# Taking one semaphore wait away from the 5.6 MB table copy in a hybrid attention block

## The chip, the cores and the metric

The kernel runs on one core of one Trainium2 chip. The metric is the device time of one execution in microseconds (us); lower is better. All work is float32: the large products are made as three products of split operands (high times high, high times low, low times high).

## The reference, cut to what matters

One decoder layer over 512 positions of width 1024. A conditioning vector gives shift, scale and gate; a normalised, modulated input `h` goes through one wide projection `w_in`, whose columns feed three attention branches; these are gated, merged, projected, and a SwiGLU mixer follows.

```python
c_act = jax.nn.silu(c)
mod = (c_act @ w_ada[l] + b_ada[l])[:, None, :]
sh1, sc1, gt1, sh2, sc2, gt2 = jnp.split(mod, 6, axis=-1)
h = rmsnorm(x, g_norm1[l]) * (1 + sc1) + sh1
(a_q, a_kv, i_q, i_k, i_w, b_q, b_k, b_v, c_q, c_k, c_v,
 z_a, z_b, z_c) = split_cols(h @ w_in[l], IN_SPLITS)
...
bias = jnp.moveaxis(bias_tab[rel_bucket(dist)], -1, 0)
logits = jnp.einsum('bqhmd,bshmd->bmhqs', qb, k) * ATTN_SCALE + bias
```

The bias depends only on the distance of query and key. So a table of a head is one row of values, laid out so that each partition reads it shifted by one.

## The kernel before, in words

**The program.** Each engine has its own instruction stream, and they meet at semaphores. SyncE (SP) issues nearly all loads, GpSimd (POOL) the few constants and the bias rows. The order on each engine is written out by hand.

**Weights.** Weights come in chunks of 1 MB (`w_raw`, two buffers, 1024 rows of 1 KB each). For each chunk ScalarE makes the high part (`make_hi`, L1143), VectorE the low part (`make_lo`, L1438), and TensorE multiplies (`project`, L762 to L764). A buffer is loaded anew (L504) when the low part of the chunk that was in it is made. Chunk 0 is the first column block of `w_in` that is used, chunks 1 to 5 follow, and chunk n+2 takes the place of chunk n. Chunk 2 is smaller (two loads).

**The start.** SP issues, without a wait: six small vectors (L510), `x` in two loads (L512), sixteen loads of 512 KB of `w_ada` (L517), chunk 0, chunk 1. All these are in one hardware queue and are worked off in order. VectorE sums the `w_ada` rows scaled by `c_act` (L1457), TensorE turns the sums into columns (L780), and then:

- ScalarE: `make_hi(0)`, then the eight high parts of `h` (L1173), then `make_hi(1)`
- VectorE: `make_lo(0)`, then shift and scale columns, then for each of eight slices of `h` the full value (L1473) and its low part (L1478, which raises `h_ready`), then `make_lo(1)`
- TensorE: tile 0 of chunk 0, slice by slice as `h_ready` rises, then the other tiles of chunks 0, 1 and 2, then chunk 3

So neither `h` nor the first projection begins before chunk 0 has landed.

**The bias tables.** TensorE makes 24 rows by a small product with a one-hot matrix (L791), ScalarE copies them to SBUF (`brow`, L1166). POOL stores them in DRAM as one flat row of 11264 values (`row_dram`, four DMAs, L676) and waits until they have landed. Then it copies that row 128 times in DRAM (`rep_dram`, L680, 5.6 MB, one DMA in the software queue). Much later, from L550 on, SP reads tables out of the copies with a pitch of one row less one element. The next instruction of POOL after the copy is `power(2, ...)` (L669), which serves the key latents.

Of the kernel before, what the change touches and what calls it, by code (L numbers as in the profile page):

```python
# [25 lines left out]
KT = D // P  # L26
# [171 lines left out]
def hybrid_block(nc, a, out):  # L198
# [7 lines left out]
    def sem(name):  # L206
        return ctx.enter_context(nc.semaphore(name))

    with ctx:
# [175 lines left out]
        h_ready = sem("h_ready")  # L385
# [262 lines left out]
        def _(pool):  # L648
# [27 lines left out]
                pool.dma_start(row_dram[0, f0:f0 + n * w].rearrange("(n w) -> n w", w=w), brow[r0:r0 + n, c0:c0 + w]) \  # L676
                    .then_inc(rows_stored, 16)
            pool.wait_ge(rows_stored, 16 * 4)
            pool.wait_ge(h_ready, KT)
            pool.dma_start(rep_dram, row_dram.to_broadcast([P, FL_W])).then_inc(rows_copied, 16)  # L680
            power(2, rs_kv, ms_kv, 4)

# [59 lines left out]
        def _(pe):  # L742
# [243 lines left out]
            def project_z(v):  # L986

                if chunk_starting_at(v) is not None:
                    chunk_ready(chunk_starting_at(v))
                (_, n), kts = dense_at(v)  # L990
                project((CH_Z + n // 2) % 2, ATT_TILE["z", n], h_hi, h_lo, [(k, k) for k in kts], n % 2 * P,
                        first=0 in kts, last=KT - 1 in kts)
# [938 lines left out]
```

## Time and profile before

| what | value |
|---|---|
| runs | 1055.12, 1054.15, 1052.42 us |
| median | 1054.15 us |
| profiled execution, own time | 1055.12 us |
| its span | 1053.0 us |
| TensorE busy | 1000.0 us, 95% |
| VectorE, ScalarE, GpSimd busy | 484.5, 412.4, 115.7 us |
| mean granted TensorE clock | 0.983 |
| moved by the DMA engines | 121.49 MB |

The profile is of one execution. "PE" is TensorE, "DVE" VectorE, "ACT" ScalarE. The span runs from the first to the last instruction; the execution's own time has 2.1 us more around it. The whole kernel is one stream of TensorE work after about 45 us, so a time at which TensorE starts or stalls counts more than the busy share of any other engine.

### The profile page before, as it was taken

How to read it: one execution, taken by the hardware profiler on the slowest of the kernel's cores; microseconds unless marked ns; L12 is line 12 of the kernel's file. 1: busy time of each engine (PE TensorE's matmuls, PEld its weight loads, DVE VectorE, ACT ScalarE, POOL GpSimd, SP SyncE). 2: the span in 40 equal slices, each digit the busy share in tenths (PEclk: the TensorE clock that was granted, in tenths of full speed). 3: DMA queues.
4: the chain of work that ended last, by engine and by line, in shares of the span. 5: the costliest groups of instructions: out<-in, count | busy, mean ns of one | idle time of the engine just before them, and what ended most of it. 6: DMA issues, size and time to landing. Idle time of an engine off the chain costs nothing.

```text
span 1053.0 us, 12662 instructions
## 1 busy us (share of the span) xinstructions
PE 1000.0 (95%) x4831; PEld 809.4 (77%) x4831; DVE 484.5 (46%) x803; ACT 412.4 (39%) x676; POOL 115.7 (11%) x136
## 2 busy tenths in 40 slices
PE   2799999999999999999999999799999999999997
PEld 0677988878877766778888888588888888788886
DVE  3845687833235344553746567623233232322331
ACT  4434523255455655642222222433344433412231
POOL 3000000000044411200000026300000000001111
PEclk9799999999999999999999999899999999999999
DMA  8693134312130201155556583032322323223302
GB/s 305 223 295 119 51 116 139 113 48 81 61 102 21 72 21 31 34 177 175 169 176 211 197 282 115 3 120 80 120 80 81 118 84 115 70 80 110 110 31 80
DMA packets 93262, 121.49 MB, mean 115 GB/s; under 512 B 4680, under 2 KB 83109, under 8 KB 93090
## 3 DMA queue, kind: packets, MB, share of 16 engines
q1 hardware_dynamic: 92690, 114.67, 33.0%
q0 software_dynamic: 528, 6.22, 2.0%
q8 instruction: 29, 0.48, 0.2%
q14 instruction: 15, 0.12, 0.0%
HBM read 118.20 MB, written 8.45 MB: 120 GB/s over the span
## 4 chain that ended last, share of the span: by engine, by line
PE 86%; DMA 4%; DVE 4%; ACT 2%; SPq 2%; issue 1%; POOL 0%; POOLq 0%; DVEq 0%; ACTq 0%
PE tile_ps L762 24%; PE tile_ps L764 23%; PE tile_ps L763 23%; DMA w_raw<-in_w_in_dram 4%; PE s_ps L902 2%; PE t_ps L920 2%; PE o_ps L949 2%; SPq L517 2%; DVE w_lo L1438 1%; ACT w_hi L1143 1%; PE s_ps L905 1%; PE tile_ps L963 1%; PE tile_ps L1008 1%; PE tile_ps L969 1%; PE tile_ps L1009 1%
## 5 line engine op out<-in xcount | busy, mean ns | idle before, releaser
L762 PE MATMUL tile_ps<-h_hi,w_hi 128*128 128x512 f32 x816 | 326.9, 401 | 13.1 <-DVE h_lo L1845 4.3
L764 PE MATMUL tile_ps<-h_hi,w_lo 128*128 128x512 f32 x816 | 320.3, 393 | 0.0
L763 PE MATMUL tile_ps<-h_lo,w_hi 128*128 128x512 f32 x816 | 319.9, 392 | 0.0
L1438 DVE TENSOR_TENSOR w_lo<-w_raw,w_hi 128x2048 fp32r<-128x2048 f32 (+2 forms) x78 | 172.3, 2209 | 249.0 <-ACT w_hi L1143 249.0
L762 PEld LDWEIGHTS tile_ps<-h_hi,w_hi 128*128 128x128 f32 x816 | 153.9, 189 | 58.2 <-issue 16.7
L764 PEld LDWEIGHTS tile_ps<-h_hi,w_lo 128*128 128x128 f32 x816 | 153.9, 189 | 33.5
L1143 ACT ACTIVATE w_hi<-w_raw 128x2048 fp32r<-128x2048 f32 (+2 forms) x78 | 143.8, 1844 | 89.9 <-PE tile_ps L764 68.7
L763 PEld LDWEIGHTS tile_ps<-h_lo,w_hi 128*128 128x128 f32 x816 | 154.3, 189 | 29.9
L762 PE MATMUL tile_ps<-f_hi,w_hi 128*128 128x512 f32 x176 | 69.1, 393 | 2.5 <-DVE f_lo L1862 2.5
L764 PE MATMUL tile_ps<-f_hi,w_lo 128*128 128x512 f32 x176 | 69.2, 393 | 0.0
L763 PE MATMUL tile_ps<-f_lo,w_hi 128*128 128x512 f32 x176 | 69.1, 393 | 0.0
L1266 ACT ACTIVATE nl<-nl,cst 128x256 f32<-128x256 f32 (+3 forms) x81 | 43.0, 532 | 55.4 <-DVE cst L1609 55.3
L1401 ACT ACTIVATE f_hi<-f_t 128x512 f32 x22 | 13.9, 633 | 95.5 <-DVE f_t L1858 95.5
L722 POOL TENSOR_TENSOR sq_acc<-x 128x512 f32<-128x512 f32 x2 | 2.1, 1042 | 442.2 <-DVE x L1872 267.6
L693 POOL TENSOR_TENSOR tm<-tab,score 128x256 f32<-128x256 f32 (+2 forms) x24 | 24.4, 1015 | 175.1 <-DVE cst L1609 175.1
L1858 DVE TENSOR_TENSOR f_t<-tile_ps,silu_t 128x512 f32<-128x512 f32 x22 | 15.2, 692 | 60.2 <-PE tile_ps L764 60.2
L1278 ACT ACTIVATE pt<-t_ps 128x128 f32<-128x128 f32 (+2 forms) x80 | 32.1, 402 | 27.1 <-PE t_ps L920 26.5
L762 PEld LDWEIGHTS tile_ps<-f_hi,w_hi 128*128 128x128 f32 x176 | 33.5, 190 | 9.8 <-DVE f_lo L1862 2.9
L764 PEld LDWEIGHTS tile_ps<-f_hi,w_lo 128*128 128x128 f32 x176 | 33.4, 190 | 7.0
L763 PEld LDWEIGHTS tile_ps<-f_lo,w_hi 128*128 128x128 f32 x176 | 33.4, 190 | 7.0
L1396 ACT ACTIVATE silu_t<-tile_ps 128x512 f32<-128x512 f32 x22 | 13.2, 600 | 46.2 <-PE tile_ps L764 46.1
L1609 DVE CUSTOM_DVE_ANT_0 nl<-s_ps,tm 128x256 f32<-128x256 f32 (+2 forms) x24 | 13.4, 557 | 36.6 <-PE s_ps L902 36.4
(272 smaller groups left out, 1354.1 us busy)
## 6 DMA issues: line engine op xcount, KB each, us to landing
w_raw<-in_w_in_dram SPq DMA_DIRECT2D x31, 1024.0 KB, 5.5
w_raw<-in_w_gate_up_dram SPq DMA_DIRECT2D x22, 1024.0 KB, 5.1
ada<-in_w_ada_dram SPq DMA_DIRECT2D x16, 1024.0 KB, 5.7
ada<-in_w_ada_dram SPq DMA_DIRECT2D x16, 512.0 KB, 15.4
w_raw<-in_w_down_dram SPq DMA_DIRECT2D x8, 1024.0 KB, 5.2
row_copies<-row_flat POOLq DMA_DIRECT2D x1, 5632.0 KB, 21.2
w_raw<-in_w_out_dram SPq DMA_DIRECT2D x4, 1024.0 KB, 9.6
tab<-row_copies SPq DMA_DIRECT2D x12, 256.0 KB, 2.7
```

The lines of the kernel that those rows point to most:

```text
L517: sp.dma_start(ada1[g][k][:], a["w_ada"][0][k * P:(k + 1) * P, g * D:(g + 1) * D]) \
L693: pool.tensor_tensor(tm[v % 2][:, 0:w], table_of(v), score[:, off:off + w], ALU.add) \
L762: pe.matmul(tile_ps[b][0:mw, :], wh, x_hi[:, kx, :], start=start, stop=False)
L763: pe.matmul(tile_ps[b][0:mw, :], wh, x_lo[:, kx, :], start=False, stop=False)
L764: mm = pe.matmul(tile_ps[b][0:mw, :], wl, x_hi[:, kx, :], start=False, stop=stop)
L902: mm = pe.matmul(ps[:, 0:w], qlat[h % 2][:, i * P:(i + 1) * P], kv_T[:, 0:w], start=True, stop=True)
L920: mm = pe.transpose(t_ps[v % 2][:, j * P:(j + 1) * P], src[:, j * P:(j + 1) * P], ident[:])
L949: mm = pe.matmul(o[:, i * P:(i + 1) * P], kv_nat[:, j, :], p_j, **flags)
L1143: nc.scalar.activation(w_hi[s][:, 0:kt, :], w_raw[s][:, 0:kt, :], ACT.Copy).then_inc(w_hi_made[s], 1)
L1266: act.activation(b, b, ACT.Exp, bias=negmax[:, k:k + 1], scale=-1.0, accum_out=expsum[:, k:k + 1]).then_inc(exped, 1)
L1278: act.activation(pt[v % 2][:, 0:w], t_ps[v % 2][:, 0:w], ACT.Copy).then_inc(pt_ready, 1)
L1438: dve.tensor_tensor(w_lo[s][:, 0:kt, :], w_raw[s][:, 0:kt, :], w_hi[s][:, 0:kt, :].bitcast(F32), ALU.subtract) \
```

## The change

The copy of the flat row no longer waits until all eight slices of `h` are ready. It is issued as soon as the four stores of the row have landed.

```diff
             pool.wait_ge(rows_stored, 16 * 4)
-            pool.wait_ge(h_ready, KT)
             pool.dma_start(rep_dram, row_dram.to_broadcast([P, FL_W])).then_inc(rows_copied, 16)
             power(2, rs_kv, ms_kv, 4)
```

## Rows read from the trace of the kernel before

**Rows 1.** The page: busy time; chain by engine; loads of `w_in`, KB, us to landing.
```profile
PE 1000.0 (95%) x4831; PEld 809.4 (77%) x4831; DVE 484.5 (46%) x803; ACT 412.4 (39%) x676; POOL 115.7 (11%) x136
...
PE 86%; DMA 4%; DVE 4%; ACT 2%; SPq 2%; issue 1%; POOL 0%; POOLq 0%; DVEq 0%; ACTq 0%
...
w_raw<-in_w_in_dram SPq DMA_DIRECT2D x31, 1024.0 KB, 5.5
```

**Rows 2.** Chain of waits, 0 to 140 us: start, duration, what.
```profile
20.52 17.63 DMA w_raw<-in_w_in_dram
...
40.12 2.29 DVE w_lo L1438
42.74 0.56 DVE x_T L1473
...
55.25 22.39 DMA w_raw<-in_w_in_dram
...
81.96 0.50 PE tile_ps L762
```

**Rows 3.** Timeline: start, duration, instruction, idle time before and its releaser.
```profile
26.61 2.30 POOL L676 DMA_DIRECT2D row_flat<-brow  x4 [6.02 <-ACT brow L1166]
...
38.18 1.91 ACT L1143 ACTIVATE w_hi<-w_raw 128x2048 fp32r<-128x2048 f32 x1 [4.75 <-DMA w_raw<-in_w_in_dram]
...
44.82 0.76 PE L762 MATMUL tile_ps<-h_hi,w_hi 128*128 128x512 f32 x1 [4.18 <-DVE h_lo L1478]
...
51.00 1.90 ACT L1143 ACTIVATE w_hi<-w_raw 128x2048 fp32r<-128x2048 f32 x1
...
52.36 0.55 POOL L680 DMA_DIRECT2D row_copies<-row_flat  x1 [23.45 <-DVE h_lo L1478]
```

**Rows 4.** The four row stores, L676, by their line.
```profile
L676 POOL DMA_DIRECT2D row_flat<-brow x4: 499/521/777, 26.6 to 28.4; - x4
...
DMA to landing us min/median/max: 4.6/4.7/5.0
```

**Rows 5.** The copy, L680, by its line.
```profile
DMA to landing us min/median/max: 21.2/21.2/21.2
```

**Rows 6.** DMA queue, 34.4 to 42 us: packets, MB, share of 16 engines.
```profile
q1 hardware_dynamic: 1772, 1.78, 73.7%
```

**Rows 7.** DMA queues, 53 to 71.9 us.
```profile
q0 software_dynamic: 128, 5.77, 92.3%
q1 hardware_dynamic: 80, 0.08, 5.5%
```

**Rows 8.** Hardware queue, 71.9 to 75 us, then 75 to 76.2 us.
```profile
q1 hardware_dynamic: 508, 0.52, 82.1%
...
q1 hardware_dynamic: 439, 0.44, 105.8%
```

**Rows 9.** TensorE's waits, 20 to 180 us: total, times, longest.
```profile
PE tile_ps L762 <- DVE h_lo L1478: 4.2, 1, 4.2
PE o_ps L780 <- DVE ada_sum L1457: 2.7, 1, 2.7
PE tile_ps L762 <- DVE w_lo L1438: 1.4, 1, 1.4
```

**Rows 10.** Timeline of ScalarE, 60 to 110 us.
```profile
70.18 0.59 ACT L1183 ACTIVATE iq_split<-tile_ps 64x512 fp32r<-64x512 f32 x1
77.66 1.92 ACT L1143 ACTIVATE w_hi<-w_raw 128x2048 fp32r<-128x2048 f32 x1 [6.89 <-DMA w_raw<-in_w_in_dram]
...
109.87 0.28 ACT L1217 ACTIVATE junk<-o_ps 128x128 f32<-128x128 f32 x1
```

**Rows 11.** Stages: length, busy time of each engine, granted clock, DMA share, GB/s.
```profile
44.00:48.00 4.00, 3.18 (x8) 2.53 (x9) 4.00 (x8) 2.36 (x4) 0.00 (x0) 0.50 0.76 194
48.00:49.00 1.00, 1.00 (x4) 0.79 (x3) 1.00 (x3) 0.63 (x1) 0.00 (x0) 0.63 0.00 0
```

**Rows 12.** Timeline of SyncE's queue, the first read of the copies.
```profile
175.35 2.34 SPq L550 DMA_DIRECT2D tab_near<-row_copies  x1
```

## The prediction

> **What bounds the kernel now.** I read the page first. TensorE is busy 95% of the span, and 86% of the chain that ended last is TensorE's [rows 1]. For almost any change outside TensorE the answer would then be "nothing". The exception is the time before TensorE has anything to multiply, and the removed wait acts just there. So I went next to the chain of waits of the first 140 us. The reader is to see two transfers in it [rows 2]. The load of chunk 0 is issued at 20.52 and lands 17.63 us later, at 38.15. Its high part, low part, the first slice of `h` and TensorE's first product follow without a gap: 38.18, 40.12, 42.74 and 44.82 [rows 2, 3]. The second is the load of chunk 3, issued at 55.25, which takes 22.39 us and lands at 77.64; TensorE starts on that chunk at 81.96. TensorE's waits of this stretch say what each costs: it waited 4.2 us for `h` at the start, and 1.4 us for the low part of chunk 3 [rows 9]. From there to 180 us it waited for nothing else.
>
> Third come the DMA queues, stretch by stretch. They show what the copy does to a load that is in flight with it. From 53 to 71.9 us the software queue, which then holds only the copy, works off 128 packets of 45 KB, 8 on each of the 16 engines. The hardware queue, which has chunk 3 waiting since 55.25 and chunk 4 behind it, works off 80 packets of 1 KB, 5 on each engine [rows 7]. A DMA engine that has both queues takes about one packet from each in turn, and one of 45 KB against one of 1 KB is no sharing at all. A packet of the copy occupies its engine 0.923 x 18.9 / 8 = 2.18 us. When the copy is through, the 1 KB packets move at full speed: 508 in the 3.1 us in which the last engines leave the copy, then 439 in 1.2 us, or 366 per us [rows 8]. This is why chunk 3 took 22.39 us.
>
> **The change part by part.** It removes a wait and adds nothing. What moves is one DMA issue.
>
> Step 1, when the copy is issued. The last of the four stores is issued at 28.4 and lands 4.7 us later (4.6 to 5.0), at 33.1 [rows 4]. The copy goes out then instead of at 52.36 [rows 3], which is 19.3 us earlier. Before, its first packets ran some 1.3 to 2 us after the issue (issue 52.36, all 128 start between 53 and 71.9 us [rows 7]). So they now begin at about 34.4, and it lands 21.2 us after the issue [rows 5], at 54.3.
>
> Step 2, what it meets. At 34.4 the hardware queue still has 1772 packets to send [rows 6]. Two chunks are 2 x 1024 packets of data and 2 x 16 that signal, 2080 together, so 308 are gone and chunk 0 has 1040 - 308 = 732 left, 46 for each engine. The `w_ada` packets are ahead of these and are through.
>
> Step 3, what chunk 0 gets. While the copy runs, one packet for each of the 8 packets of the copy on each engine: 128. Left over are 604. I move the rows of before by the 19.3 us. At 71.9 - 19.3 = 52.6 us the copy's packets have all started; 508 go in the next 3.1 us and the other 96 in 0.3 us, so the data ends at 56.0. For chunk 3 the same sum gives 960 packets left at 71.9, hence an end at 76.2 us, and it landed at 77.64: 1.4 us from the last data to landing. Chunk 0 lands at 57.4. If the slow 3.1 us are an accident and the 604 go at 366 per us, the data ends at 54.3 and it lands at 55.7. I take 57.2, close to the measured stretch. Against 38.15 that is 19.0 us late, with 17.5 and 19.3 as the ends.
>
> Step 4, what is behind it. `make_hi(0)` stands ahead of the high parts of `h` on ScalarE, and `make_lo(0)` ahead of the shift, scale and `h` work on VectorE, so all of it moves by the same 19.0 us: TensorE starts its first tile at 44.8 + 19.0 = 63.8. The cover for the lateness of chunk 0 is zero, since the chain runs through it [rows 2]. The sum for the two `w_ada` halves, for which TensorE waited 2.7 us [rows 9], ends before 41 us as before and no longer matters. TensorE's clock was granted at 0.50 from 44 to 48 us (the lower of 1.2 and 2.4 GHz) and rose between 48 and 49, about 3.8 us after TensorE had started [rows 3, 11]. It now stands idle for longer before the start, and the clock cannot be lower. I put no change on this. If it rises 2 us sooner or later after the start than it did, TensorE works 2 us more or less at half the rate, which is 1 us either way.
>
> Chunk 1 is next in the queue: 1040 packets at 366 per us are 2.8 us, landing at about 60. ScalarE wants it at 51.0 + 19.0 = 70.0 [rows 3]. Nothing waits there.
>
> Step 5, what the change gives back. Chunk 3 is now issued at 55.25 + 19.0 = 74.3, when the copy is 20 us gone, and takes some 5.5 us, the median of the loads of `w_in` [rows 1]. ScalarE can make its high part as soon as it is through with L1183, at 70.8 on the old clock, instead of at 77.66 [rows 10], VectorE the low part 4 us later, before TensorE is done with chunk 2. The 1.4 us of waiting [rows 9] go. Nothing else of the start was waiting for a transfer [rows 9], so this is the whole gain. It can be nothing at worst, if TensorE then meets another wait at that place.
>
> Step 6, downstream. The tables are first read at 175.35 [rows 12], 100 us after the copy had landed; making it earlier is worth nothing there. POOL's `power(2)`, which stands behind the copy, waits for squares that ScalarE makes at 109.87 [rows 10]. No slack after 64 us takes up a late start: TensorE works through, and its loads follow its own pace.
>
> Sum: +19.0 - 1.4 = +17.6 us. Ends: 17.5 - 1.4 - 1 = +15.1, and 19.3 - 0 + 1 = +20.3. The profiled execution took 1055.12 us, which gives 1072.7; it is the slowest of three, and the median is 1054.15. I forecast against the median: 1071.8, with ends at 1069.3 and 1074.5, and 2 us more on the low side and 1.5 on the high side for the runs' own spread of 2.7 us.
>
> **The rivals.**
>
> Several small packets in one turn. Chunk 3's packets were sent one to a turn [rows 7], but they were queued after the copy had begun. Chunk 0's are in the queue ahead of it, and may be fetched in groups. From six to a turn on it matters, since 46 are then through before the 8 turns are. At twelve to a turn, four turns of the copy (8.7 us) and the 46 packets' own 2.0 us come first: data to 45.1, landed at 46.5, +8.4 - 1.4 = +7.0, or 1061. Against it: 80 packets to 96 of the copy that ran beside them. The Trainium skill, "DMA: Bandwidth & Descriptors", section "Queues, rings and completion order", says that an engine goes round the queues by whole packets of typically 9 to 17 descriptors. By that rule, if each small record of this trace is one descriptor, chunk 0 would need six turns down to three, and the estimate is +11 to +5 us. The trace does not agree with such groups for the 1 KB rows. Chance 0.08.
>
> Sharing by bytes. If the engines gave each queue half of the bytes, chunk 0's 732 packets (2.0 us alone) would take 4.0 us: +2.0 - 1.4 = +0.6, or 1054.8, no change. What speaks for it is only that chunk 3's case began the other way round. Against it are 5.77 MB to 0.08 MB [rows 7]. Chance 0.05.
>
> The other side: chunk 0 is not held up at all, because its 46 packets on each engine are already taken in when the copy's first one comes. Then only the stall at chunk 3 goes: -1.4, or 1052.8, within what can't be told from no change. This decides from 46 packets taken in ahead on every engine, at which point the whole 17 us fall away; some ten would change little. No row shows how far an engine takes in ahead. Chance 0.04.
>
> That the copy isn't earlier after all: the wait on `h_ready` ended 23.45 us of POOL's idling [rows 3], and the stores behind it had long landed [rows 4], so it was what held the copy. Chance 0.01.
>
> **How the numbers follow.** The forecast has 0.82, the rivals 0.08, 0.05, 0.04 and 0.01. The range of 1067 to 1076 is the forecast's own and leaves out less than 2 in 10. About 0.3%, 3.2 us, is what a measurement of this kernel tells from no change. Slower by more than that are the forecast and the first rival, 0.90; within it the two small cases and the last, 0.09; faster 0.01, for a gain beyond the 1.4 us that I can't name.
>
> **What would show it.** The copy's issue at about 33 us instead of 52; 128 large packets from about 34 to 53 us, and in that stretch of the order of 130 small ones in the hardware queue (step 3; 700 would mean the second or third rival, some hundreds the first); ScalarE's wait for chunk 0 grown from 4.75 us [rows 3] to about 24; TensorE's first product at about 64; chunk 3 landing some 5.5 us after its issue, and no wait of TensorE for its low part (step 5); the distance from TensorE's first product to the end shorter by 1.4 us. I would be wrong most of all if an engine holds many packets of one queue in hand, or if the copy itself ran at another speed against a full queue.

## The result, and the profile after

The changed kernel takes 1066.3 us in the median of 4 timed runs (1062.2 to 1067.9); the kernel before, beside it, 1053.99 (1052.42 to 1055.12). The ratio is 1.011, with a 95% interval of 1.008 to 1.0141: slower by 12 us. The direction was forecast (slower, 0.90). The size was not: 1071.8 was forecast, with 1067 to 1076 as the range, and the median lies 0.7 us below it. The spread is also new: all 14 executions of this kernel in that job lie between 1060.65 and 1069.22.

The profiled execution took 1068.17 us, one of the slower ones, against 1055.12 for the one of before. Its chain of waits (start, duration, what), beside [rows 2]:

```profile
20.13 34.88 DMA w_raw<-in_w_in_dram
55.03 1.92 ACT w_hi L1142
56.98 2.29 DVE w_lo L1437
59.59 0.56 DVE x_T L1472
...
61.68 0.77 PE tile_ps L761
```

The load of chunk 0, 17.63 us before, takes 34.88 us and lands at 55.01 instead of 38.15, 16.9 us late. The steps behind it have their old lengths, and TensorE's first product comes at 61.68 instead of 44.82 [rows 3], 16.9 us late as well. (Lines past the edit are one lower than before.)

The waits of TensorE from 0 to 180 us, beside [rows 9]: the wait for `h` is 17.2 us longer, and the 1.4 us for the low part of chunk 3 is gone.

```profile
PE tile_ps L761 <- DVE h_lo L1477: 21.4, 1, 21.4
...
PE o_ps L779 <- DVE ada_sum L1456: 2.6, 1, 2.6
```

The timeline of POOL, beside [rows 3], and the copy's row among the DMA issues of 0 to 120 us (KB, us to landing), beside [rows 5]. The copy goes out at 32.97 and takes 22.8 us instead of 21.2:

```profile
26.23 2.29 POOL L676 DMA_DIRECT2D row_flat<-brow  x4 [6.02 <-ACT brow L1165]
32.97 0.54 POOL L679 DMA_DIRECT2D row_copies<-row_flat  x1 [4.46 <-DMA row_flat<-brow]
```

```profile
row_copies<-row_flat POOLq DMA_DIRECT2D x1, 5632.0 KB, 22.8
```

Now the DMA queues, stretch by stretch: 34.5 to 38, then 38 to 54, then 54 to 55.2 us. The first line of a stretch has all packets and how many are small; those under 512 B are signal packets, by which an engine reports that its share of a load is through, 16 for a load.

```profile
DMA packets 882, 1.59 MB, mean 455 GB/s; under 512 B 15, under 2 KB 866, under 8 KB 866
q1 hardware_dynamic: 866, 0.87, 78.8%
q0 software_dynamic: 16, 0.72, 48.7%
...
DMA packets 224, 5.16 MB, mean 323 GB/s; under 512 B 0, under 2 KB 112, under 8 KB 112
q0 software_dynamic: 112, 5.05, 96.0%
q1 hardware_dynamic: 112, 0.11, 3.7%
...
DMA packets 136, 0.12 MB, mean 103 GB/s; under 512 B 15, under 2 KB 136, under 8 KB 136
q1 hardware_dynamic: 122, 0.12, 34.4%
```

How the 16.9 us become 13.05. The first L825 transposes, behind the first tile of chunk 3, start at 102.8 (87.6 before): +15.2, so 1.7 us came back at chunk 3. The distance stays 15.2 up to 400 us and is 13.2 at the first transposes of the output (1053.3, L1121, against 1040.1). TensorE waits there for the same things and as long, to 0.3 us; what differs is the granted clock. These are the stretches in question, kernel before, then after (length, busy times, granted clock, DMA share, GB/s):

```profile
380.00:400.00 20.00, 18.10 (x82) 12.49 (x81) 10.52 (x33) 10.99 (x28) 2.89 (x5) 0.92 0.13 41
...
917.00:925.00 8.00, 6.26 (x21) 5.02 (x22) 3.66 (x4) 2.43 (x2) 0.00 (x0) 0.79 0.21 66
```

```profile
395.00:415.00 20.00, 18.10 (x93) 12.81 (x94) 10.71 (x33) 11.60 (x29) 2.87 (x5) 1.00 0.14 41
...
930.00:940.00 10.00, 7.53 (x34) 5.91 (x33) 4.28 (x4) 2.43 (x2) 0.00 (x0) 1.00 0.19 67
```

The execution of before had two short drops of the clock; the one of after had none there. They are not tied to the change: another profile of the changed kernel (the first one below) has both drops, with a granted clock of 0.91 from 395 to 415 us and 0.83 from 920 to 930 us. These 2 us are luck of the profiled pair.

### The profile page after: what moved, and what is told of

Its sections match the earlier page's. It is cut to its first block, busy times and chain, and to the rows that moved or that the text cites. A ratio compares the mean times of both kernels' runs of the same rounds, so it can differ in the third digit from the quotient of the medians.

```text
span 1066.2 us, 12661 instructions
## 1 busy us (share of the span) xinstructions
PE 997.5 (94%) x4831; PEld 808.3 (76%) x4831; DVE 484.5 (45%) x803; ACT 412.5 (39%) x676; POOL 115.5 (11%) x136
## 4 chain that ended last, share of the span: by engine, by line
PE 88%; DMA 3%; DVE 2%; ACT 2%; SPq 2%; issue 1%; POOL 0%; POOLq 0%; DVEq 0%; ACTq 0%
PE tile_ps L761 25%; PE tile_ps L763 24%; PE tile_ps L762 24%; DMA w_raw<-in_w_in_dram 3%; PE s_ps L901 2%; PE o_ps L948 2%; PE t_ps L919 2%; SPq L517 1%; PE s_ps L904 1%; PE tile_ps L962 1%; PE tile_ps L1007 1%; PE tile_ps L968 1%; PE tile_ps L1008 1%; PE tile_ps L1009 1%; DVE w_lo L1437 1%
## 5 line engine op out<-in xcount | busy, mean ns | idle before, releaser
L1857 DVE TENSOR_TENSOR f_t<-tile_ps,silu_t 128x512 f32<-128x512 f32 x22 | 15.2, 692 | 60.2 <-PE tile_ps L763 60.2
L1395 ACT ACTIVATE silu_t<-tile_ps 128x512 f32<-128x512 f32 x22 | 13.2, 600 | 46.3 <-PE tile_ps L763 46.2
L1608 DVE CUSTOM_DVE_ANT_0 nl<-s_ps,tm 128x256 f32<-128x256 f32 (+2 forms) x24 | 13.4, 557 | 36.6 <-PE s_ps L901 36.5
## 6 DMA issues: line engine op xcount, KB each, us to landing
row_copies<-row_flat POOLq DMA_DIRECT2D x1, 5632.0 KB, 22.8
```

The source lines that it names most:

```text
L1857: dve.tensor_tensor(f_t[:, m, :], tile_ps[m][:], silu_t[:, m, :], ALU.mult) \
```

## The experiments

**Theory A**, formed on the profile after: it is a race. The copy's first packets come several us after its issue, when the hardware queue is full. What an engine has not sent of a load by then goes out at one packet a turn, 2.2 us each. The load lands with the engine that is furthest behind. **Theory B** is the prediction's: hundreds of packets of chunk 0 are left at the copy's start, on all engines.

**The changed kernel again.** No edit. Two more profiles of it, besides that of the result.

> The changed kernel once more, unaltered. Theory A (the race of the last packets): in the profile of the changed kernel 15 of the 16 signal packets of chunk 0 were sent before the copy's first packets, and one engine's only after its last. Whether and how long chunk 0 is held is then decided by the engine that is furthest behind, and it lands between turns of the copy: at 38 us if all engines are through, else at about 38 + 2.2 n, up to 55 to 56. So I expect another landing of chunk 0 in this profile than 55.0 with even chance, the first product of TensorE 6.65 us after it, and a spread of the times of several us against under 3 for the kernel before. Theory B (the prediction's: hundreds of packets of chunk 0 are left when the copy begins): chunk 0 always lands 1 to 3 us behind the copy, within 1 us from run to run.

> The changed kernel once more, for a third profile of it. Theory A: chunk 0 lands between 38 and 56 us at a turn of the copy (two profiles showed 42.9 and 55.0), chunk 1 always 1 to 3 us behind the copy's last packets, near 59; the time is about 1061 if chunk 0 lands within the first three or four turns, since chunk 1 then sets it, and above that goes up with the landing of chunk 0 to 1069. A landing of chunk 0 behind the copy's end with hundreds of its packets left would speak for theory B.

The first: 1065.2 us in the median, runs of 1061.37, 1061.38, 1069.03 and 1069.25 against 1050.56 to 1056.03 for 19 runs of the kernel before. Timeline of ScalarE (chunk 0, chunk 1), then TensorE's waits:

```profile
42.88 1.91 ACT L1142 ACTIVATE w_hi<-w_raw 128x2048 fp32r<-128x2048 f32 x1 [9.31 <-DMA w_raw<-in_w_in_dram]
59.08 1.92 ACT L1142 ACTIVATE w_hi<-w_raw 128x2048 fp32r<-128x2048 f32 x1 [3.29 <-DMA w_raw<-in_w_in_dram]
```

```profile
PE tile_ps L761 <- DVE h_lo L1477: 8.0, 1, 8.0
...
PE tile_ps L761 <- DVE iq_split L1494: 3.4, 1, 3.4
```

The second (1061.5 us), the same rows, and its DMA packets of 34.5 to 38 and of 38 to 40 us:

```profile
39.21 1.91 ACT L1142 ACTIVATE w_hi<-w_raw 128x2048 fp32r<-128x2048 f32 x1 [6.58 <-DMA w_raw<-in_w_in_dram]
58.10 1.91 ACT L1142 ACTIVATE w_hi<-w_raw 128x2048 fp32r<-128x2048 f32 x1 [5.98 <-DMA w_raw<-in_w_in_dram]
```

```profile
PE tile_ps L761 <- DVE iq_split L1494: 6.0, 1, 6.0
PE tile_ps L761 <- DVE h_lo L1477: 5.9, 1, 5.9
```

```profile
DMA packets 797, 1.51 MB, mean 430 GB/s; under 512 B 15, under 2 KB 781, under 8 KB 781
...
DMA packets 32, 0.74 MB, mean 368 GB/s; under 512 B 1, under 2 KB 16, under 8 KB 16
```

One kernel, and chunk 0 lands at 55.0, 42.9 and 39.2. In the last case too 15 signals are out when the copy begins, but the 16th goes with the next turn. In the middle one it goes with the second turn, between 41.5 and 42 us. Theory B is dead: it had chunk 0 behind the copy each time. The profiles also show what the prediction had not seen. When chunk 0 gets through early, chunk 1 does not; it lands at 58 to 59 instead of 41, and TensorE waits 3.4 or 6.0 us for it (the row names VectorE's last instruction before; ScalarE's row above shows the DMA). So +4.7 us at the first product is +6.4 behind chunk 3, and +1.0 is +8.3.

**The copy twice.**

```diff
             pool.dma_start(rep_dram, row_dram.to_broadcast([P, FL_W])).then_inc(rows_copied, 16)
+            pool.dma_start(rep2_dram, row_dram.to_broadcast([P, FL_W])).then_inc(copied_again, 16)
```

> The copy is made a second time, into another DRAM tensor, straight behind the first; the tables wait for both. The software queue is then full of 45 KB packets for some 40 us instead of 20. Theory A: the engine that was behind has only a few packets of chunk 0 more than the turns of one copy, so chunk 0 lands between 55 and 72 us, before the second copy (about 76), and chunk 1, of which every engine has 65 packets left, lands behind the second copy at about 78 to 80. Theory B: each engine has 38 packets of chunk 0 left after the first copy and gets 8 more sent during the second, so chunk 0 lands at 76 to 78, some 21 us later than now, and the kernel takes about 1088.

1081.01 us in one run. Chunk 0 and chunk 1 on ScalarE:

```profile
54.78 1.91 ACT L1146 ACTIVATE w_hi<-w_raw 128x2048 fp32r<-128x2048 f32 x1 [22.55 <-DMA w_raw<-in_w_in_dram]
77.16 1.91 ACT L1146 ACTIVATE w_hi<-w_raw 128x2048 fp32r<-128x2048 f32 x1 [9.46 <-DMA w_raw<-in_w_in_dram]
```

(The edit also gives the second copy its tensor and its semaphore, for which the first read of the tables waits.) As A said, and not B: the second copy did not move chunk 0, which had hardly a packet more to send than the first copy had turns, and moved chunk 1 by some 19 us. (54.8 and 77.2 are a little under A's lower ends of 55 and 78. In this profile 13 signals of chunk 0 were out when the copy began, not 15: three engines had some left.)

**Holding the copy back.** One or two small power operations of POOL ahead of the issue.

```diff
             pool.wait_ge(rows_stored, 16 * 4)
+            for n in range(2):      # in the other kernel: once
+                pool.tensor_tensor(spare, ones[:, 0:4], half[:, 0:4], ALU.pow).then_inc(idled, 1)
+                pool.wait_ge(idled, n + 1)
             pool.dma_start(rep_dram, row_dram.to_broadcast([P, FL_W])).then_inc(rows_copied, 16)
```

> Between the landing of the row stores and the issue of the copy POOL makes two small power operations on a spare column, some 3 to 4 us in all, so the copy is issued at about 36.5 instead of 33. Theory A: by the time of its first packets every engine is through with chunk 0, which lands at 38.2 as in the kernel before, TensorE's first product is at 44.8; the engine furthest behind in chunk 1 is caught instead, chunk 1 lands at about 58 to 60 instead of 41, its low part is ready some 4 us after TensorE wants it at 58.5, and 1.4 us come back at chunk 3: about +3, or 1057. Theory B: the copy is 3.5 us later, so chunk 0 still has more than a hundred packets left and lands 1 us after the copy, at 58: about +17, or 1071.

> The copy is issued after one small power operation of POOL, at about 34.5 to 35, between the changed kernel (33, chunk 0 caught by one engine) and the kernel with two such operations (36.1, nothing caught). Theory A (the race): the first packets come at 38 to 38.5, every engine is through with chunk 0, which lands at 38 (a late engine may cost a turn or two, 2.2 us each), and chunk 1, of which 20 to 40 packets are left on each engine, lands behind the copy at 57 to 59. TensorE then waits some 7 us before the first tile of chunk 1 and no more for chunk 3: +6 to +8 in all, 1060 to 1062, with a spread as small as that of the kernel before. Rival (chunk 0's delay and chunk 1's go together, both set by the traffic of the copy): chunk 0 lands at a turn between 40 and 57 as before and the time is 1061 to 1069.

(`spare` and `idled` are a column and a semaphore made for this.) With two: issue at 36.14, chunk 0 at 37.4, and no wait of ScalarE for chunk 1, which was expected to be caught and was not. The time is 1053.77 (10 runs), a ratio of 0.9994 (0.9981 to 1.0008). The step that I had wrong was again when the copy's first packets come: between 38.5 and 40, when chunk 1 was sent too. How they come says why they are late. These are the stretches 38.5 to 39, 39 to 39.5 and 39.5 to 40 us of this kernel:

```profile
DMA packets 145, 0.49 MB, mean 985 GB/s; under 512 B 8, under 2 KB 137, under 8 KB 137
q0 software_dynamic: 8, 0.36, 170.0%
...
DMA packets 59, 0.32 MB, mean 637 GB/s; under 512 B 6, under 2 KB 53, under 8 KB 53
q0 software_dynamic: 6, 0.27, 126.1%
...
DMA packets 14, 0.10 MB, mean 201 GB/s; under 512 B 2, under 2 KB 12, under 8 KB 12
q0 software_dynamic: 2, 0.09, 41.9%
```

The 16 signals of chunk 1 come as 8, 6 and 2, and so do the copy's first 16 packets. An engine starts on the copy when it is through with all that it had of chunk 1, without taking turns for what was queued ahead. Against an empty queue (below) the copy's packets were there some 1.3 us after the issue, which here is 37.4; every engine first sent what it had in hand. (That the 8, 6 and 2 are the same engines is read from the counts; the trace doesn't name them.)

With one: issue at 35.06, first packets from 38.5 on, 1062.72 us (1061.58 to 1063.66), 0.7 us above what I expected, ratio 1.0096 (1.0077 to 1.0116). Seven engines were through with chunk 1 too (7 signals from 38.5 to 39.5). Its ScalarE rows and TensorE's first wait:

```profile
37.82 1.91 ACT L1146 ACTIVATE w_hi<-w_raw 128x2048 fp32r<-128x2048 f32 x1 [4.79 <-DMA w_raw<-in_w_in_dram]
58.15 1.91 ACT L1146 ACTIVATE w_hi<-w_raw 128x2048 fp32r<-128x2048 f32 x1 [7.42 <-DMA w_raw<-in_w_in_dram]
```

```profile
PE tile_ps L765 <- DVE iq_split L1498: 7.6, 1, 7.6
```

Chunk 0 on time, chunk 1 caught, and 1.1 us between the issues of the two kernels are worth 9 us. Four runs of the one lie within 2.1 us. Why a wait of 3.4 us costs less than one of 6 or 7.6 is in the granted clock, from 66 to 68 us in this kernel and in the first repetition (the number behind the five busy times):

```profile
66.00:68.00 2.00, 2.00 (x6) 1.54 (x6) 1.64 (x3) 1.15 (x1) 0.00 (x0) 0.50 0.45 160
```

```profile
66.00:68.00 2.00, 1.50 (x7) 1.29 (x8) 1.73 (x3) 1.98 (x2) 0.00 (x0) 1.00 0.94 333
```

After the 7.6 us the clock is at the lower of its two levels (1.2 GHz) and stays there into the stretch of 68 to 70; after the 3.4 us it never left the upper one. In sums: from the first product to behind chunk 3 this kernel lost 7.4 us more than the kernel before, where 7.6 us of waiting less the 1.7 us that come back at chunk 3 make 5.9, so the clock cost some 1.5. The same sum gives some 3 us for the 6.0 us of the kernel's third profile and next to nothing for the 3.4 us.

**The first two loads swapped.**

```diff
-            load(0, [(KT, 0, cols(COL_IQ, CW))])
             load(1, [(KT, 0, cols(COL_IQ + CW, CW))])
+            load(0, [(KT, 0, cols(COL_IQ, CW))])
```

> The changed kernel with the first two loads in the other order: chunk 1, then chunk 0. Now it is chunk 1 that has only its last packets left when the copy begins, and chunk 0 has all or nearly all of its 65 packets on every engine. This is the case that the prediction had in mind. Theory A: chunk 0 lands 2 to 3 us behind the copy's last packets every time, at 58 to 59, the first product of TensorE comes 6.65 us later at 64.5 to 65.5, nothing waits for chunk 1 or 3: +18 to +19, 1072, and the spread of the runs is small, under 4 us, since no race decides it. Rival (the spread of the changed kernel comes from the copy itself, which is faster or slower from run to run): the spread stays at 8 us.

1074.39 us (1070.25 to 1075.3), ratio 1.0196 (1.0167 to 1.0226). Chunk 0 on ScalarE, TensorE's wait:

```profile
57.74 1.91 ACT L1142 ACTIVATE w_hi<-w_raw 128x2048 fp32r<-128x2048 f32 x1 [25.59 <-DMA w_raw<-in_w_in_dram]
```

```profile
PE tile_ps L761 <- DVE h_lo L1477: 24.3, 1, 24.3
```

This is the case that the prediction had worked out, a load with most of its packets behind the copy's start, and its sum holds here up to chunk 3: the landing was put at 57.2 to 57.4 and is 57.7, and the profile is +19.6 at the first product and +18.1 behind chunk 3. The time is above it: +21.3 against the kernel before beside it (1053.06), where the sum had +17.6 and +20.3 at most, and 2.4 us above what I expected of this run. The spread is 5 us, not under 4; three of the runs lie within 1.3 us at a granted clock of 0.972, the fourth is 4 us shorter at 0.979. The expectation on the spread is therefore not borne out with four runs, and this experiment doesn't decide what the spread comes from.

**Small packets.** The copy as eleven DMAs of 1024 columns, at the early place and at the old one. (The first read of the tables waits for all eleven.)

```diff
-            pool.dma_start(rep_dram, row_dram.to_broadcast([P, FL_W])).then_inc(rows_copied, 16)
+            for f0 in range(0, FL_W, 1024):
+                pool.dma_start(rep_dram[:, f0:f0 + 1024], row_dram[:, f0:f0 + 1024].to_broadcast([P, 1024])) \
+                    .then_inc(rows_copied, 16)
```

> The copy at the early place, but as eleven DMAs of 1024 columns, so that its packets are 4 KB instead of 45 KB (1408 of them, 88 on each engine). If an engine takes one packet of each queue in turn (theories A and B alike) then a packet of chunk 0 waits 0.2 us instead of 2.2. Under A a few packets are left on one engine and chunk 0 lands by 40; under B 46 on each, which take 46 turns of 0.24 us, 11 us, landing at 47. In both the load of chunk 3 is no longer held up. A: 1053 to 1055. B: 1061. The rival to both, that an engine stays with the copy's queue until it is empty whatever the packets' size: chunk 0 lands at 55 as now, 1066.

> The kernel before with the copy at its late place, but in eleven pieces with packets of 4 KB instead of 45 KB. One packet of each queue in turn (theory A) gives the load of chunk 3 one of its 65 packets per engine each 0.25 us: it lands at about 72 instead of 77.6, before TensorE needs it, and the stall of 1.4 us at chunk 3 is gone: 1052 to 1053. If packets' size did not matter, chunk 3 would land at 77.6 and the time be that of the kernel before, 1053.7.

Early: 1055.32 us (10 runs, 1050.59 to 1058.07), ratio 1.0012 (0.9995 to 1.0029). Chunk 0 landed at 39.5, chunk 1 at 54.9, and TensorE waited 2.6 us for the latter. The two queues from 38 to 43 us:

```profile
q0 software_dynamic: 437, 1.59, 77.9%
q1 hardware_dynamic: 438, 0.45, 25.6%
```

Again one for one, now with packets of 4 KB: the same turns. The early copy now costs some 1.6 us, and the interval includes no cost at all. (A had 1055 as its upper end and chunk 0 by 40; that chunk 1 would still be held up I had not seen.) Late: 1051.71 us (11 runs), ratio 0.9984 (0.9975 to 0.9993), but chunk 3 landed at 76.4 only, not at 72, and a wait of 0.8 us was left. From 63 to 73 us it got 758 packets, 76 per us. I had reckoned with a packet each 0.25 us on an engine, which is 64 per us; the rate is met, but the load's first packets started more than 3.4 us after its issue at 54.55 (none before 58), behind the copy's. By 73 us the hardware queue had sent 994 packets, nearly a load's 1040, and chunk 3 landed 3.4 us later: the engines that were last were late. So the time was met and the landing was not; the wait at chunk 3 shrank by 0.6 us, and the rest of the 1.9 us gained is not explained by it.

**Other places for the copy.** POOL waits for the landing of chunk 0, or of chunk 1.

```diff
             pool.wait_ge(rows_stored, 16 * 4)
+            pool.wait_ge(w_loaded[0], 16)      # in the other kernel: w_loaded[1]
             pool.dma_start(rep_dram, row_dram.to_broadcast([P, FL_W])).then_inc(rows_copied, 16)
```

> The copy waits for the landing of chunk 0 (38.2) instead of for h_ready (52.4). Theory A (what counts is which packets are still unsent when the copy's first ones go out): chunk 0 can't be held, and chunk 1, whose last packets leave by 40.5, is through or nearly. The copy runs from about 40 to 60. Chunk 2, issued at 42.4, is now what it holds up: it lands at about 63 instead of 50, its low part is ready at 67 to 68, TensorE wants it at 69.6, so nothing waits. Chunk 3 is behind it and lands by 67 instead of 77.6; the stall of 1.4 us at chunk 3 goes. 1052 to 1053, 1.4 us under the kernel before. Rival (an early copy costs by its traffic, whatever it overlaps): slower by some us.

> The copy waits for the landing of chunk 1 (about 41), so that both queues are empty when it is issued. Theory A: its first packets come 1.3 us after the issue, as in the kernel before (with a full queue it was 3.6 to 4 us). Chunk 2, issued 1.4 us later, gets one packet a turn until about 61 and lands at 65 to 66 (2048 packets), its low part is ready at about 70.5 and TensorE wants it at 69.6: a stall of 0 to 1.5 us there against 1.4 us less at chunk 3. 1052.5 to 1054.5. Rival (the time from issue to the first packet is the software queue's own, full or empty): first packets 3.5 us after the issue here too.

Both came as expected. Behind chunk 0: 1052.26 us (11 runs), ratio 0.9987 (0.9978 to 0.9996). Behind chunk 1: 1054.32 (12 runs), ratio 1.0008 (0.9995 to 1.0021), with 1.7 us of waiting for chunk 2 in the place of the 1.4 us for chunk 3. Chunk 2 on ScalarE in the two kernels:

```profile
63.53 1.92 ACT L1143 ACTIVATE w_hi<-w_raw 128x2048 fp32r<-128x2048 f32 x1 [4.34 <-DMA w_raw<-in_w_in_dram]
```

```profile
64.67 1.92 ACT L1143 ACTIVATE w_hi<-w_raw 128x2048 fp32r<-128x2048 f32 x1 [5.99 <-DMA w_raw<-in_w_in_dram]
```

An early copy is cheap where the load that it holds up has slack, and 1.1 us later on ScalarE that slack is used up. With the queues empty its first packet came 1.2 to 1.3 us after the issue (issue 40.70, first packet between 41.9 and 42.0), so the 3.8 us and more are not the software queue's own.

## Why the prediction was wrong in its size

**Where the copy goes out.** Right: 33.1 forecast, 32.97 measured.

**When its first packets come.** This is the step that failed, the second half of step 1: "So they now begin at about 34.4". It carried over the 1.3 to 2 us that the copy took against an empty hardware queue. Against a full one the first packet came 3.8 to 4.0 us after the issue, in all six profiles that issued it between 32.6 and 34.3 us; in the profiled execution that is 36.8, not 34.4. From 34.4 to 36.8 us the hardware queue of the kernel before sends 827 packets, more than the 732 that step 2 had left of chunk 0. So by the prediction's own count nothing of chunk 0 would have been left on an average engine, and its 19.0 us had no ground. The experiments, by the time of issue and the half microsecond in which the first packets fall:

| kernel | issue | first packets | chunk 0 on ScalarE | TensorE's wait for chunk 1 |
|---|---|---|---|---|
| changed | 32.97 | 36.5 to 37 | 55.03 | none |
| changed, third profile | 32.71 | 36.5 to 37 | 39.21 | 6.0 us |
| changed, second profile | 34.24 | 38 to 38.5 | 42.88 | 3.4 us |
| one operation held | 35.06 | 38.5 to 39 | 37.82 | 7.6 us |
| two operations held | 36.14 | 38.5 to 39 | 37.41 | none |
| behind chunk 0 | 38.35 | 39.5 to 40 | 37.84 | none |
| behind chunk 1 | 40.70 | 41.5 to 42 | 37.34 | 0, and 1.7 us for chunk 2 |

**What is left of chunk 0 then** (step 2). Forecast 732 packets, 46 on each engine. Measured: 15 of 16 signals out, hence one engine that lacks some. In the three profiles it lacked one turn's worth, two turns' or eight and more. That it is one engine is read from the count of signals (three engines in the kernel that copies twice); the trace doesn't tell packets by engine, so which one, and why it was behind, is open. "46 for each engine" took the engines as level, and this is the prediction's second miss, a term that it put at nothing: in the kernel before the signals of chunk 0 lie 1.7 us apart, and the engines are apart before that. (33 signals stand among the 1772 packets of [rows 6], not 32, so that one engine was still on `w_ada` at 34.4. That these packets "are through" was off by two; nothing in the sum hangs on them.)

**One packet of each queue in a turn** (step 3). Right, and shown with 45 KB packets (112 to 112) and with 4 KB ones (437 to 438). The Trainium skill, "DMA: Bandwidth & Descriptors", section "Queues, rings and completion order", has an engine go round its queues packet by packet. By that rule, with one record of these 1 KB loads as one packet, the rows agree. Its typical 9 to 17 descriptors in a packet, which I had turned into a rival, no run here shows for them.

**The landing of chunk 0.** Forecast 57.2; measured 55.0, 42.9 and 39.2. That the profiled execution came within 2.2 us of the forecast is luck: eight packets left on one engine wait for the end of the copy as 46 on every engine would. So is that the median lies only 0.7 us below the range, since it is a mixture of such cases. The sum was right for a load with most of its packets left, which the swapped loads show: 57.7.

**From landing to first product** (step 4). Right: 6.6 to 6.7 us in all profiles. "Nothing waits there", of chunk 1, was right only where chunk 0 was the later one. Where chunk 0 slipped through, chunk 1 landed at 58 to 59 against a need at 51 to 56, and set a floor of some 7 us. That is why no execution of the changed kernel came near 1053, and it fits that the times lie from about 1061 (in the profiles, chunk 1 in charge) up to 1069 (chunk 0); for executions without a profile this is not shown.

**What comes back at chunk 3** (step 5). Forecast 1.4 us; 1.7 us came. **Downstream** (step 6): nothing was taken up, right; what the profiles differ by there is the granted clock.

**The rivals.** The one that I had called the other side, the 46 packets taken in ahead, had 0.04. It had the right mechanism for 15 engines, and its time, 1052.8, was wrong for two reasons: a load counts as landed with its last engine, and the 16th is not through. The next load in the queue is then the one that is caught, which I had priced for the forecast only. How much an engine has in hand can be estimated: 3.9 us against a full queue less 1.3 us against an empty one are 2.6 us, and at 827 packets in 2.4 us on 16 engines that is some 56 packets of 1 KB for each, more than the 46. The other reading, that the copy itself only becomes ready late, does not fit the kernel with two operations held, where the copy's first packets follow each engine's last one of chunk 1, 8, 6 and 2 of them in three stretches. Whether what bounds the 56 is a number of packets or something else that takes 2.6 us, the runs don't tell.

Two of the kernels beat both: behind chunk 0 (0.9987), by the 1.4 us that the stall at chunk 3 had cost, and the late copy in 4 KB pieces (0.9984), by 1.9 us, of which the shorter stall is 0.6. Both intervals exclude 1, but both gains are under the 0.3% set for a difference that counts.
